# Norm statistics of six stage openings: on 128 token partitions, spread by a diagonal and a matmul of ones

## The chip, the cores and the metric

The kernel runs on one core of one Trainium2 chip. The metric is the device time of one execution in microseconds (us). It is one large program: three transformer-like blocks behind one another on 512 tokens of 1024 channels, in float32, with each weight product made from two float32r parts (a high part and the rest).

## What is computed

Each block is a chain of mixer and feed-forward stages, and most of them open with a root-mean-square norm over the 1024 channels of a token, often followed by a modulation with a shift and a scale:

```python
def rms_norm_3(x, w):
    xf = x.astype(jnp.float32)
    y = xf * lax.rsqrt(jnp.mean(xf * xf, axis=-1, keepdims=True) + EPS)
    return (y * w.astype(jnp.float32)).astype(x.dtype)

def modulate(h, shift, scale):
    return h * (1 + scale) + shift
```

At the seam from the second to the third block two norms follow one another: the second block ends with `norm_f_w_2`, and the third opens with `norm1_w_3` on its result.

## The kernel before

The residual x lies in on-chip memory as `core.x`, 128 partitions x 8 channel tiles x 512 tokens: channels are on partitions, tokens in the free dimension. The stage ahead of a norm leaves `core.sumsq` (128 x 512), the squares of x added over the 8 channel tiles; what is still missing is the sum over the 128 partitions. (The first mixer makes its squares itself, from x as it is loaded.)

Six stages open with such a norm: the first mixer (`stage_first_mixer`), the three feed-forward stages (`stage_ffn`; called FFN1, FFN2 and FFN3 here), the opening of the second block (`stage_delta_rows`, called delta) and the opening of the third block (`stage_third_begin`, called begin). The first five use the class `Norm`, begin has the same steps written out for its two norms. The steps of `Norm`, by engine:

- TensorE (PE), L415: a matmul of a 128 x 128 matrix of ones with `sumsq`. It sums over the partitions and leaves the sum of each token on all 128 partitions, in PSUM (128 x 512, `acc`). A float32 matmul shows as two records in the trace. Behind it `keep_warm` (L290) issues 6 or 7 more matmuls of constants, whose result nobody reads. They have no waits.
- VectorE (DVE), L463 and L465: mean plus epsilon, then the reciprocal, both on 128 x 512.
- ScalarE (ACT), L428: the square root, on 128 x 512.
- DVE, L474: for each of the 8 channel tiles k, x times the gain times `rstd`, into one of three buffers; ACT, L434 or L436, makes the high part of the stage's input from it, and DVE, L447 or L449, the low part. DVE's order is scale 0, scale 1, low part 0, scale 2, low part 1, and so on. Each low part raises `lesser`.
- PE then waits for `lesser` tile by tile and works off the first two weight pieces (`pair`, L278), six matmuls for each channel tile. From there on it goes on through the stage's other pieces.

Each engine works in the order of its own program. ACT has other work ahead of the square root: it makes the high parts (L368) of the first weight pieces, 2 or 4 of them, each as soon as its load has landed. GpSimd (POOL) makes the low parts of the same pieces (L375), each 128 x 1024, and reads them from on-chip memory. Between two stages POOL also clears the semaphores of the stage that has ended. All stages end with a barrier of all engines.

In begin, PE sums `sumsq` and `sumsq2` (L2956, L2957), DVE works the two norms together (L3027 to L3034), and ACT takes the root (L2987). `root` serves the opening of the third block; the second statistic, `gains`, is inverted (L3045) and rooted (L2993) behind the 8 channel tiles, and used later, when x itself is scaled. PE's order is the two sums, `keep_warm`, the pair of `rows_.tensor(2)`, then `gates.tensor(0)` (L2838), then the next rows. ACT's order behind the 8 high parts is two weight pieces, the root of `gains`, and only then `rows_.scalar(1)`, which takes the first result of the pair out of PSUM.

## Time and profile before

| | us |
|---|---|
| median of 3 runs | 3575.83 |
| lowest, highest | 3573.02, 3578.72 |
| span of the profiled execution | 3572.5 |

The three runs are the timed ones; the profiled execution has a span of its own, from its first to its last instruction, and no other time is listed for it. The profile's page gives the busy time of each engine, the chain of waits and the groups of instructions. The timeline gives single instructions or runs of equal ones: start, duration, engine, line, operation and, in square brackets, how long the engine had been idle and what ended that. The stretches (windows) give busy times and the clock granted to TensorE, where 1.00 is 2.4 GHz and 0.50 is 1.2 GHz.

### The profile page before, as it was taken

Reading aid. Unit: us, or ns where it says so; the run is one execution under the profiler, and the core shown is the slowest. Engines: PE = TensorE matmul, PEld = TensorE weight load, DVE = VectorE, ACT = ScalarE, POOL = GpSimd, SP = SyncE. Lnnn points to the kernel's source line nnn. Section 1 sums busy time; section 2 is a strip of 40 time slices with the busy share of each in tenths; the row PEclk is TensorE's granted clock in tenths of the full one; section 3 lists DMA queues with packets and bytes.
Section 4 is the critical chain, followed back from the end, with each engine's and each line's share of the span. In section 5 each row is a group of like instructions: output and inputs, shape, how many; then the busy total and the mean of one; then the engine's idle time right before and its main releaser. Section 6 shows DMA issues by size and latency. Waiting matters only on the chain. (4 is left out here: it accounts for less than half of the span.)

```text
span 3572.5 us, 44627 instructions
## 1 busy us (share of the span) xinstructions
PE 3280.6 (92%) x17750; PEld 2615.2 (73%) x17750; DVE 2137.5 (60%) x2499; ACT 1255.3 (35%) x1906; POOL 1363.7 (38%) x625
## 2 busy tenths in 40 slices
PE   8999999999998899989999998979988758799997
PEld 5778777888766678967888867757876536678885
DVE  6586775889755575344746474867973677531012
ACT  4333433323244323233323342333432544332222
POOL 3434353444332234333444343326631222334442
PEclk9999999999999999999999999989999878899999
DMA  3223353474332246353444132423324555422322
GB/s 118 89 89 126 119 189 117 161 250 153 114 126 83 92 133 167 117 173 136 143 158 140 61 120 98 147 81 125 102 103 129 172 152 162 136 83 83 106 86 68
DMA packets 237262, 447.06 MB, mean 125 GB/s; under 512 B 59792, under 2 KB 119888, under 8 KB 230272
## 3 DMA queue, kind: packets, MB, share of 16 engines
q1 hardware_dynamic: 229984, 433.73, 37.5%
q10 hardware_dynamic: 7072, 10.49, 0.8%
q8 instruction: 141, 2.31, 0.3%
q14 instruction: 65, 0.53, 0.1%
HBM read 394.78 MB, written 49.37 MB: 124 GB/s over the span
## 5 line engine op out<-in xcount | busy, mean ns | idle before, releaser
L375 POOL TENSOR_TENSOR third_feed_lo<-third_feed_raw,third_feed_hi 128x1024 fp32r<-128x1024 f32 (+3 forms) x191 | 449.2, 2355 | 801.0 <-ACT third_feed_hi L368 783.0
L375 POOL TENSOR_TENSOR second_feed_lo<-second_feed_raw,second_feed_hi 128x1024 fp32r<-128x1024 f32 (+3 forms) x182 | 405.6, 2230 | 656.9 <-ACT second_feed_hi L368 627.7
L375 POOL TENSOR_TENSOR first_feed_lo<-first_feed_raw,first_feed_hi 128x1024 fp32r<-128x1024 f32 (+4 forms) x182 | 394.8, 2173 | 560.4 <-ACT first_feed_hi L368 550.6
L273 PE MATMUL shared_ps<-third_h_hi,third_feed_hi 128*128 128x512 f32 (+1 forms) x776 | 324.2, 418 | 55.5 <-ACT lgate_rows_out L894 11.9
L274 PE MATMUL shared_ps<-third_h_lo,third_feed_hi 128*128 128x512 f32 (+1 forms) x776 | 312.5, 403 | 0.0
L275 PE MATMUL shared_ps<-third_h_hi,third_feed_lo 128*128 128x512 f32 (+1 forms) x776 | 312.3, 402 | 0.0
L368 ACT ACTIVATE third_feed_hi<-third_feed_raw 128x1024 fp32r<-128x1024 f32 (+3 forms) x191 | 190.6, 1001 | 297.2 <-PE ffn_low L275 79.1
L368 ACT ACTIVATE second_feed_hi<-second_feed_raw 128x1024 fp32r<-128x1024 f32 (+3 forms) x182 | 173.9, 956 | 206.6 <-PE ffn_low L275 70.8
L368 ACT ACTIVATE first_feed_hi<-first_feed_raw 128x1024 fp32r<-128x1024 f32 (+4 forms) x182 | 168.7, 929 | 209.8 <-PE mixer_acc L275 80.5
L273 PE MATMUL mixer_acc<-first_h_hi,first_feed_hi 128*128 128x512 f32 x544 | 220.5, 405 | 7.5 <-DVE first_h_lo L1578 4.8
L273 PEld LDWEIGHTS shared_ps<-third_h_hi,third_feed_hi 128*128 128x128 f32 (+1 forms) x776 | 152.3, 196 | 100.8 <-issue 64.7
L537 DVE SCALAR_TENSOR_TENSOR ffn_ada_sum<-ffn_ada_w,cond,ffn_ada_sum 128x512 f32<-128x512 f32 x196 | 219.2, 1134 | 4.0
L275 PE MATMUL mixer_acc<-first_h_hi,first_feed_lo 128*128 128x512 f32 x544 | 213.0, 392 | 0.0
L274 PE MATMUL mixer_acc<-first_h_lo,first_feed_hi 128*128 128x512 f32 x544 | 212.8, 391 | 0.0
L725 DVE TENSOR_TENSOR ffn_mid_lo<-ffn_gate,ffn_mid_hi 128x512 fp32r<-128x512 f32 x66 | 113.3, 1716 | 120.8 <-ACT ffn_mid_hi L661 119.4
L274 PEld LDWEIGHTS shared_ps<-third_h_lo,third_feed_hi 128*128 128x128 f32 (+1 forms) x776 | 152.5, 197 | 32.9 <-issue 2.5
L275 PEld LDWEIGHTS shared_ps<-third_h_hi,third_feed_lo 128*128 128x128 f32 (+1 forms) x776 | 151.5, 195 | 33.9
L273 PE MATMUL scans_ps<-delta_in_h_hi,second_feed_hi 128*128 128x512 f32 (+1 forms) x376 | 155.5, 414 | 14.0 <-PEq L1937 6.1
L274 PE MATMUL scans_ps<-delta_in_h_lo,second_feed_hi 128*128 128x512 f32 (+1 forms) x376 | 150.1, 399 | 0.0
L275 PE MATMUL scans_ps<-delta_in_h_hi,second_feed_lo 128*128 128x512 f32 (+1 forms) x376 | 149.9, 399 | 0.0
L273 PE MATMUL ffn_acc<-first_h_hi,first_feed_hi 128*128 128x512 f32 x352 | 138.4, 393 | 1.9 <-DVE first_h_lo L447 1.9
L273 PE MATMUL ffn_acc<-second_h_hi,second_feed_hi 128*128 128x512 f32 x352 | 137.4, 390 | 1.4 <-DVE second_h_lo L449 1.4
(773 smaller groups left out, 8024.5 us busy)
## 6 DMA issues: line engine op xcount, KB each, us to landing
third_feed_raw<-in_stream SPq DMA_DIRECT2D x156, 512.0 KB, 3.4
second_feed_raw<-in_stream SPq DMA_DIRECT2D x130, 512.0 KB, 3.5
first_feed_raw<-in_stream SPq DMA_DIRECT2D x120, 512.0 KB, 3.3
ffn_ada_w<-in_w_ada SPq DMA_DIRECT2D x48, 1024.0 KB, 5.3
shared_seg<-scratch_cum SPq DMA_DIRECT2D x32, 512.0 KB, 7.2
scratch_gates<-mixer_gate ACTq DMA_DIRECT2D x32, 256.0 KB, 2.1
mix_gin<-scratch_gates SPq DMA_DIRECT2D x32, 256.0 KB, 3.1
first_feed_raw<-in_stream SPq DMA_DIRECT2D x28, 256.0 KB, 3.2
```

What stands on the lines that cost most here:

```text
L273: nc.tensor.matmul(out, w_hi, x_hi, start=start, stop=False)
L274: nc.tensor.matmul(out, w_hi, x_lo, start=False, stop=False)
L275: return nc.tensor.matmul(out, w_lo, x_hi, start=False, stop=stop)
L368: self.nc.scalar.activation(self.hi[:, p % self.cut, :n], self.raw[:, p % self.deep, :n], ACT.Copy).then_inc(self.cut_hi, 1)
L375: eng.tensor_tensor(self.lo[:, p % self.cut, :n], self.raw[:, p % self.deep, :n], self.hi[:, p % self.cut, :n].bitcast(F32), ALU.subtract) ...
L537: v.scalar_tensor_tensor(out=at, in0=w, scalar=by, in1=at, op0=ALU.mult, op1=ALU.add).then_inc(self.summed, 1)
L725: v.tensor_tensor(mid_lo[:, f % HALF], gate[:, f % 2], mid_hi[:, f % HALF].bitcast(F32), ALU.subtract).then_inc(done_mid, 1)
```

## The change

The sum over partitions is taken the other way round. `token_sums` makes four matmuls for the four groups of 128 tokens: `sumsq` of the group is now the stationary matrix and a single column of ones is streamed, so the sums of 512 tokens arrive as 128 x 4, tokens on partitions. DVE's mean and reciprocal and ACT's root work on 128 x 4 (`small`). Then `diagonal` multiplies the identity (128 x 128, read for each of the four groups) by `small` (each value read 128 times), a DVE operation of 128 x 512, and a matmul of ones with that diagonal puts the statistic of every token on all partitions again, in `acc` in PSUM. DVE's scaling reads `acc` in place of `rstd` in on-chip memory.

PE's queue gets a wait for the diagonal (`turned`) between two groups of `keep_warm` of two matmuls each, in place of the 6 or 7 in a row. Each norm gets two more semaphores. In begin both statistics go this way: the opening's diagonal as in `Norm`; that of `gains` is made by DVE behind scale 1, its matmul of ones stands on PE behind the pair and ahead of `gates.tensor(0)`, and ACT copies the result out of PSUM at the place where it took the root.

```diff
+def token_sums(nc, core, to, squares):
+    for c in range(4):
+        last = nc.tensor.matmul(to[:, c:c + 1], squares[:, c * P:(c + 1) * P], core.ones[:, 0:1], start=True, stop=True)
+    return last
+
+def diagonal(nc, core, to, by):
+    return nc.vector.tensor_tensor(to.rearrange("p (c t) -> p c t", c=4), core.ident[:].unsqueeze(1).broadcast_to([P, 4, P]),
+                                   by.unsqueeze(2).broadcast_to([P, 4, P]), ALU.mult)
 class Norm:
-    def tensor(self, pe):
+    def tensor(self, pe, warm):
-        self.nc.tensor.matmul(self.acc, self.core.ones[:], self.core.sumsq[:], start=True, stop=True
-                              ).then_inc(self.summed, 1)
+        token_sums(self.nc, self.core, self.acc, self.core.sumsq).then_inc(self.summed, 1)
+        keep_warm(self.nc, self.core, warm, 2)
+        pe.wait_ge(self.turned, 1)
+        self.nc.tensor.matmul(self.acc, self.core.ones[:], self.rstd[:], start=True, stop=True).then_inc(self.wide, 1)
+        keep_warm(self.nc, self.core, warm, 2)
...
-        self.nc.scalar.activation(self.rstd[:], self.rstd[:], ACT.Sqrt).then_inc(self.rooted, 1)
+        self.nc.scalar.activation(self.small[:], self.small[:], ACT.Sqrt).then_inc(self.rooted, 1)
...
-        v.tensor_scalar(self.rstd[:], self.acc, 1.0 / D, EPS, ALU.mult, ALU.add).then_inc(self.meaned, 1)
+        v.tensor_scalar(self.small[:], self.acc[:, 0:4], 1.0 / D, EPS, ALU.mult, ALU.add).then_inc(self.meaned, 1)
-        v.reciprocal(self.rstd[:], self.rstd[:]).then_inc(self.inverted, 1)
+        v.reciprocal(self.small[:], self.small[:]).then_inc(self.inverted, 1)
         dve.wait_ge(self.rooted, 1)
+        diagonal(self.nc, core, self.rstd[:], self.small[:]).then_inc(self.turned, 1)
+        dve.wait_ge(self.wide, 1)
...
-            v.scalar_tensor_tensor(out=to, in0=core.x[:, k], scalar=g[:, k:k + 1], in1=self.rstd[:], op0=ALU.mult,
-                                   op1=ALU.mult).then_inc(self.scaled, 1)
+            v.scalar_tensor_tensor(out=self.buf[:, k % 3], in0=core.x[:, k], scalar=g[:, k:k + 1], in1=self.acc,
+                                   op0=ALU.mult, op1=ALU.mult).then_inc(self.scaled, 1)
 stage_ffn, stage_first_mixer, stage_delta_rows
-            norm.tensor(pe)
-            keep_warm(nc, core, acc[:, 1], 7)
+            norm.tensor(pe, acc[:, 1])
 stage_third_begin, PE
+                token_sums(nc, core, ps[:, 4], core.sumsq).then_inc(summed, 1)
+                token_sums(nc, core, ps[:, 5], core.sumsq2).then_inc(summed, 1)
+                keep_warm(nc, core, ps[:, 1], 2)
+                pe.wait_ge(spread_, 1)
+                nc.tensor.matmul(ps[:, 5], core.ones[:], root[:], start=True, stop=True).then_inc(wide, 1)
+                keep_warm(nc, core, ps[:, 1], 2)
                 rows_.tensor(pe, 2)
+                pe.wait_ge(spread_, 2)
+                nc.tensor.matmul(ps[:, 4], core.ones[:], gains, start=True, stop=True).then_inc(wide, 1)
                 gates.tensor(pe, 0)
 stage_third_begin, ACT
-                act.wait_ge(inverted, 2)
-                a.activation(gains, gains, ACT.Sqrt).then_inc(rooted, 1)
+                act.wait_ge(wide, 2)
+                a.activation(gains, ps[:, 4], ACT.Copy).then_inc(rooted, 1)
 stage_third_begin, DVE, in the loop over c
+                    if c == 1:
+                        diagonal(nc, core, gains, small[:, 4:8]).then_inc(spread_, 1)
                     if c:
                         lesser_part(c - 1)
...
-                v.reciprocal(gains, gains).then_inc(inverted, 1)
```

## Rows read from the trace of the kernel before

**Rows 1.** The page, part 1: engine, busy us (share of span), instructions.

```profile
PE 3280.6 (92%) x17750; PEld 2615.2 (73%) x17750; DVE 2137.5 (60%) x2499; ACT 1255.3 (35%) x1906; POOL 1363.7 (38%) x625
```

**Rows 2.** Timeline of FFN1's opening: start, us, engine, line, operation [idle <-releaser].

```profile
582.41 1.98 PE L415 MATMUL ffn_total<-sumsq,ones 128*128 128x512 f32 x2 [2.46 <-PEq L1192]
584.19 6.16 PE L293 MATMUL ffn_ada_acc<-pick,ones 128*128 128x512 f32 x12
585.16 3.35 DVE L465 RECIPROCAL ffn_norm_rstd<-ffn_norm_rstd 128x512 f32<-128x512 f32 x1
587.80 2.35 POOL L375 TENSOR_TENSOR first_feed_lo<-first_feed_raw,first_feed_hi 128x1024 fp32r<-128x1024 f32 x1 [9.65 <-issue]
589.21 2.15 DVE L474 SCALAR_TENSOR_TENSOR ffn_norm_buf<-x_res,vec,ffn_norm_rstd 128x512 f32<-128x512 f32 x2 [0.70 <-ACT ffn_norm_rstd L428]
592.24 0.47 PE L273 MATMUL ffn_acc<-first_h_hi,first_feed_hi 128*128 128x512 f32 x1 [1.88 <-DVE first_h_lo L447]
```

**Rows 3.** Timeline of the first mixer's opening.

```profile
14.96 2.07 PE L415 MATMUL mixer_out<-sumsq,ones 128*128 128x512 f32 x2 [14.96 <-DVE sumsq L490]
20.13 4.65 POOL L375 TENSOR_TENSOR first_feed_lo<-first_feed_raw,first_feed_hi 128x1024 fp32r<-128x1024 f32 x2
22.35 1.28 ACT L428 ACT_TABLE_LOAD   x1
24.31 1.68 DVE L474 SCALAR_TENSOR_TENSOR mix_norm_buf<-x_res,vec,mix_norm_rstd 128x512 f32<-128x512 f32 x2 [3.16 <-ACT mix_norm_rstd L428]
26.87 0.47 PE L273 MATMUL mixer_acc<-first_h_hi,first_feed_hi 128*128 128x512 f32 x1 [2.64 <-DVE first_h_lo L447]
```

**Rows 4.** Timeline of delta's opening.

```profile
982.25 4.66 POOL L375 TENSOR_TENSOR second_feed_lo<-second_feed_raw,second_feed_hi 128x1024 fp32r<-128x1024 f32 x2 [21.54 <-ACT second_feed_hi L368]
983.54 1.28 ACT L428 ACT_TABLE_LOAD   x1
985.50 2.61 DVE L474 SCALAR_TENSOR_TENSOR slots_a<-x_res,delta_norm_full,slots_a 128x512 f32<-128x512 f32 x2 [1.37 <-ACT slots_a L428]
989.14 0.47 PE L273 MATMUL scans_ps<-delta_in_h_hi,second_feed_hi 128*128 128x512 f32 x1 [2.19 <-DVE delta_in_h_lo L449]
```

**Rows 5.** Timeline of begin's opening.

```profile
2061.22 4.85 POOL L375 TENSOR_TENSOR third_feed_lo<-third_feed_raw,third_feed_hi 128x1024 fp32r<-128x1024 f32 x2 [20.36 <-ACT third_feed_hi L368]
2062.53 1.28 ACT L2987 ACT_TABLE_LOAD   x1
2068.67 1.41 DVE L3040 SCALAR_TENSOR_TENSOR begin_buf<-x_res,begin_full,begin_root 128x512 f32<-128x512 f32 x2 [0.70 <-ACT begin_root L2987]
2071.11 0.77 PE L273 MATMUL shared_ps<-third_h_hi,third_feed_hi 128*128 128x512 f32 x1 [4.55 <-DVE third_h_lo L3018]
```

**Rows 6.** Timeline of FFN2's opening, then of FFN3's.

```profile
1681.51 1.42 DVE L474 SCALAR_TENSOR_TENSOR ffn_norm_buf<-x_res,ffn_norm_full,ffn_norm_rstd 128x512 f32<-128x512 f32 x2 [0.70 <-ACT ffn_norm_rstd L428]
...
3172.78 7.01 PE L293 MATMUL ffn_ada_acc<-pick,ones 128*128 128x512 f32 x12
3173.02 2.35 POOL L375 TENSOR_TENSOR third_feed_lo<-third_feed_raw,third_feed_hi 128x1024 fp32r<-128x1024 f32 x1 [5.46 <-ACT third_feed_hi L368]
3177.83 1.41 DVE L474 SCALAR_TENSOR_TENSOR ffn_norm_buf<-x_res,ffn_norm_full,ffn_norm_rstd 128x512 f32<-128x512 f32 x2 [0.70 <-ACT ffn_norm_rstd L428]
```

**Rows 7.** PE's timeline: single-column matmuls, full then half clock; two records of `keep_warm`.

```profile
970.06 1.84 PE L552 MATMUL ffn_ada_acc<-ones,ffn_ada_sum 128*128 128x1 f32 x16
974.95 2.23 PE L552 MATMUL ffn_ada_acc<-ones,ffn_ada_sum 128*128 128x1 f32 x10
1681.58 1.02 PE L293 MATMUL ffn_ada_acc<-pick,ones 128*128 128x512 f32 x2
```

**Rows 8.** Single lines over the run: durations in ns, least/median/most.

```profile
L1887 DVE TENSOR_SCALAR delta_bias<-vec x1: 164/164/164, 978.1 to 978.1; 128x4 f32<-128x4 f32 x1
L4238 DVE TENSOR_TENSOR ssm_xw<-ssm_xdt,ssm_w x24: 680/684/2852, 2771.3 to 3025.5; 128x512 f32<-128x512 f32 x24
```

**Rows 9.** A stretch of FFN1: busy times (PE to POOL), then granted clock, DMA.

```profile
592.80:595.80 3.00, 3.00 (x8) 2.34 (x7) 3.00 (x6) 1.73 (x3) 0.00 (x0) 0.50 0.08 30
```

More of the change, by code:

```diff
@@ L407, in __init__ @@
         self.rstd, self.buf = bufs
+        self.small = s.sb("norm_small", [P, 4])
+        self.turned, self.wide = owner.sem("norm_turned"), owner.sem("norm_wide")
         (self.squared, self.added, self.summed, self.meaned, self.inverted, self.rooted, self.ready, self.scaled,
@@ L427, in scalar @@
         act.wait_ge(self.inverted, 1)
-        self.nc.scalar.activation(self.rstd[:], self.rstd[:], ACT.Sqrt).then_inc(self.rooted, 1)
-        if self.parts is None:
-            return
+        self.nc.scalar.activation(self.small[:], self.small[:], ACT.Sqrt).then_inc(self.rooted, 1)
         for k in range(DT):
@@ L614, in _ @@
                 steps = 0
-                norm.tensor(pe)
-                keep_warm(nc, core, ada_acc[:], 6)
+                norm.tensor(pe, ada_acc[:])
                 for half in range(2):
@@ L1264, in out @@
                 last.then_inc(out_ready, 1)
-            norm.tensor(pe)
-            keep_warm(nc, core, acc[:, 1], 7)
+            norm.tensor(pe, acc[:, 1])
             pair(pe, feed, ROWS1[:2], norm.lesser, (acc[:, 0], acc[:, 1]), h)
@@ L1824, in lora @@
                     last.then_inc(product_, 1)
-                norm.tensor(pe)
-                keep_warm(nc, core, ps[:, 1], 7)
+                norm.tensor(pe, ps[:, 1])
                 rows_.tensor(pe, 5)
@@ L2901, in stage_third_begin @@
         k, v_ctx, last_ = s.sb("k", [P, 4, CTX]), s.sb("v_ctx", [P, 2, D]), s.sb("last", [P, 2, 4])
-        start = s.sb("start", [P, 2, 256])
+        start, small = s.sb("start", [P, 2, 256]), s.sb("small", [P, 8])
         gates = LogGates(nc, core, s, s, ps[:, 6:8].rearrange("p a (b c) -> p (a b) c", c=CTX), CTX, CTX, b)
@@ L2908, in stage_third_begin @@
         stored = [s.sem(f"stored{n}") for n in range(2)]
-        gained = s.sem("gained")
+        gained, spread_, wide = s.sem("gained"), s.sem("spread"), s.sem("wide")
         with nc.Block() as block:
@@ L2954, in state @@
                     last.then_inc(product_, 1)
-                nc.tensor.matmul(ps[:, 4], core.ones[:], core.sumsq[:], start=True, stop=True).then_inc(summed, 1)
-                nc.tensor.matmul(ps[:, 5], core.ones[:], core.sumsq2[:], start=True, stop=True).then_inc(summed, 1)
-                keep_warm(nc, core, ps[:, 1], 7)
+                token_sums(nc, core, ps[:, 4], core.sumsq).then_inc(summed, 1)
[4 more added lines that the diff above has]
+                keep_warm(nc, core, ps[:, 1], 2)
                 rows_.tensor(pe, 2)
+                pe.wait_ge(spread_, 2)
+                nc.tensor.matmul(ps[:, 4], core.ones[:], gains, start=True, stop=True).then_inc(wide, 1)
                 gates.tensor(pe, 0)
@@ L2986, in _ @@
                 act.wait_ge(inverted, 1)
-                a.activation(root[:], root[:], ACT.Sqrt).then_inc(rooted, 1)
+                a.activation(small[:], small[:], ACT.Sqrt).then_inc(rooted, 1)
                 for c in range(DT):
@@ L3026, in _ @@
                 dve.wait_ge(summed, 2)
-                v.tensor_scalar(gains, ps[:, 4], 1.0 / D, EPS, ALU.mult, ALU.add).then_inc(meaned, 1)
+                v.tensor_scalar(small[:, 4:8], ps[:, 4, 0:4], 1.0 / D, EPS, ALU.mult, ALU.add).then_inc(meaned, 1)
                 dve.wait_ge(meaned, 1)
-                v.tensor_scalar(root[:], gains, EPS, None, ALU.mult).then_inc(meaned, 1)
+                v.tensor_scalar(small[:, 0:4], small[:, 4:8], EPS, None, ALU.mult).then_inc(meaned, 1)
                 dve.wait_ge(meaned, 2)
-                v.scalar_tensor_tensor(out=root[:], in0=ps[:, 5], scalar=1.0 / D, in1=root[:], op0=ALU.mult,
-                                       op1=ALU.add).then_inc(meaned, 1)
+                v.scalar_tensor_tensor(out=small[:, 0:4], in0=ps[:, 5, 0:4], scalar=1.0 / D, in1=small[:, 0:4],
+                                       op0=ALU.mult, op1=ALU.add).then_inc(meaned, 1)
                 dve.wait_ge(meaned, 3)
-                v.reciprocal(root[:], root[:]).then_inc(inverted, 1)
+                v.reciprocal(small[:], small[:]).then_inc(inverted, 1)
                 dve.wait_ge(rooted, 1)
+                diagonal(nc, core, root[:], small[:, 0:4]).then_inc(spread_, 1)
                 dve.wait_ge(ready, 2)
+                dve.wait_ge(wide, 1)
                 for c in range(DT):
@@ L3039, in _ @@
                         dve.wait_ge(lesser, c - 2)
-                    v.scalar_tensor_tensor(out=buf[:, c % 3], in0=core.x[:, c], scalar=full[:, c:c + 1], in1=root[:],
+                    v.scalar_tensor_tensor(out=buf[:, c % 3], in0=core.x[:, c], scalar=full[:, c:c + 1], in1=ps[:, 5],
                                            op0=ALU.mult, op1=ALU.mult).then_inc(scaled, 1)
+                    if c == 1:
+                        diagonal(nc, core, gains, small[:, 4:8]).then_inc(spread_, 1)
                     if c:
```

14 lines of the change are left out of this document (5 added, 9 removed).

## Prediction

> **What bounds the kernel now.** I read the page first: TensorE (PE) is busy for 92% of the span, so a stage costs what PE needs for it plus what PE stands still [rows 1]. A norm that opens a stage is such a standstill. PE's own operation, the sum, is followed by constant matmuls that nobody needs, and the first weight matmul comes only when DVE has made the first low part: at 26.87, 592.24, 989.14 and 2071.11, each with an idle time that a low part ended [rows 2 to 5]. Behind it PE has work without a break, so what the first weight matmul comes earlier or later is what the stage ends earlier or later. I therefore follow that one instruction through six openings, in the timeline.
>
> In FFN1 the chain is plain: sum at 582.41, first scale at 589.21, 6.80 later, of which the reciprocal alone is 3.35 [rows 2]. The reader should see that the other openings are not all like this. In the first mixer and in delta the root stands behind ACT's weight pieces and its table load, which ends at 22.35 + 1.28 = 23.63 and 983.54 + 1.28 = 984.82, while the scales start at 24.31 and 985.50, only one root later [rows 3, 4]. There the reciprocal is not what comes last. In begin the table load ends at 2063.81, and the root, one root's time ahead of the scale at 2068.67, starts 4.2 later: it could move so far, not more [rows 5].
>
> **Prices of the new steps.** Four single-column matmuls are eight records. Sixteen took 1.84 at full clock (8: 0.92), ten took 2.23 at half clock (8: 1.78) [rows 7]. A DVE operation of 128x4 takes 0.164 [rows 8], so mean and reciprocal are about 0.4 with their handovers; the root of 128x4 I put at 0.2, its old 0.63 being the upper bound (the scale's start less the table's end). The diagonal is a DVE tensor_tensor of 128x512 with two on-chip operands, one of them a broadcast: the nearest row is L4238, of that form, at 0.68, but with cases of 2.85 [rows 8]. What such a case is can be seen in delta: its first two scales, two on-chip operands too, took 2.61 in place of begin's 1.41, so the first was done at about 985.50 + 0.75 + 1.20 = 987.45, which is 0.54 behind the end of POOL's low parts at 982.25 + 4.66 = 986.91 [rows 4, 5]. So bounds 0.7 free, POOL's end + 0.54 held; where POOL is at work I take held, since two forms show it. The wide matmul of ones is two records: 1.02 at full clock [rows 7], 1.98 at half [rows 2]. Between the sums and it PE has four constant records: 1.72 at full clock (1.02 less the overlap, 0.43 each), 3.4 at half.
>
> After the first scale nothing changes in size: the first low part and first weight matmul follow 2.56 later in the mixer, 2.44 in begin [rows 3, 5]. In FFN1 it was 3.03, the first scales being slowed by POOL (2.15 for two) [rows 2]. Reading `acc` from PSUM I cost at nothing.
>
> **Opening by opening.**
> - First mixer. Root at 23.65 as before, done 23.85. POOL's last low part runs to 24.78 [rows 3], so the diagonal is done at 25.3 instead of 24.6. PE, with 1.8 + 3.4 of sums and constants from 14.96 at most, has stood for five microseconds then, so I take the wide matmul at half clock: 27.4, against a first scale at 24.31 [rows 3]. Loss 3.1. Bounds: 1.3 (free, full clock) to 5.1 (half clock also through the four constants behind it, 0.5, and through three microseconds of the pair, 1.5).
> - Delta. Root done at 985.05, POOL until 986.91 [rows 4], diagonal 987.45, wide at half clock 989.4; plus 2.5 is 991.9 against 989.14. Loss 2.8; bounds 0.1 to 4.9.
> - FFN1. The constants show the clock: twelve records in 6.16 where full clock would need 5.3, so the first two ran at half, until shortly before 586 [rows 2]. New: sums to 584.2, mean and reciprocal 584.6, root 584.8 or, behind the table load, somewhat later, diagonal by 586 (POOL starts only at 587.80). But four constant records from 584.2, two at half and two at full clock, run until 586.8. Wide until 587.9: first scale 1.3 earlier. The first low part then falls under POOL's piece (587.80 + 2.35 = 590.15, about 0.2 later by more semaphores to clear), so the first weight matmul comes at 591.0: gain 1.2. In the profile the clock fell behind that gap and stayed at half from 592.8 to 595.8, which cost 1.5 [rows 9]; the constants behind the wide matmul leave a gap no longer than before's 1.88 [rows 2], so I count half of it, 0.8. Gain 2.0; bounds -0.5 to 2.8.
> - FFN2. The same without a table load and with the diagonal held until about PE's constants end: gain 1.4 of the scale's start at 1681.51 [rows 6]; bounds -0.4 to 1.8.
> - FFN3. POOL holds from 3173.02 to 3175.37, diagonal 3175.9, wide partly in the half-clock stretch that the constants show there (7.01 for twelve records, so four at half), to 3177.5 against 3177.83 [rows 6]. Gain 0.3; bounds -0.3 to 1.2.
> - Begin. Two sums; statistics done by 2061.3; root at 2063.85, done 2064.05; POOL until 2066.07 [rows 5], diagonal 2066.6, wide at half clock 2068.6: nothing gained against 2068.67. The second diagonal, in DVE's queue between scale 1 and the first low part, holds that low part and with it PE by 0.7. The pair began at half clock (0.77 for its first matmul, 0.47 elsewhere) [rows 3, 5], which for a stretch like FFN1's [rows 9] is worth 1.5; half of that, 0.7, comes back if PE is kept busy. The second wide matmul then stands on PE's own path, 1.0. Its readers, ACT's copy and the rows queued behind that, were late behind the second reciprocal before and are no later relative to PE. That reciprocal (3.35 on DVE) was hidden beside PE's pair and gives nothing. Loss 0.9 (the 0.7 for the diagonal, 1.0 for the matmul, less 0.7 and 0.1); bounds -2.3 to +2.5.
>
> Sum: -3.1 - 2.8 + 2.0 + 1.4 + 0.3 - 0.9 = -3.1, so 3.1 us slower: a span of 3575.6 against 3572.5. What lies around the span is 3.3 by the median of the runs (3575.83), which gives 3578.9. Bounds added up: 6.9 faster to 13.5 slower.
>
> **A rule on the clock.** After 4.55 us without a matmul begin's pair ran at half clock; after 2.64 in the mixer the first weight matmul (0.47, against 0.77 in begin) ran at full [rows 3, 5]. The Trainium skill, "TensorE: Matmul & The Clock Gate", section "HAM oscillation — how this bites in real kernels", says that PE which idles between bursts is throttled again, so that each burst begins cold; begin agrees, the mixer does not. By that rule alone the second rival would be the forecast.
>
> **Rivals.**
> 1. The short chain counts everywhere. If sums, four small steps, diagonal and wide were all that stood between PE's start and the first scale, at 1.8 + 0.4 + 0.3 + 0.7 + 2.0 = 5.2 at half clock or 3.4 at full against 6.8, each of six openings would gain about 2: 3564. For it: FFN1's chain, with 3.35 in one reciprocal. Against it: the table loads in mixer and delta, POOL in four of six, PE's own constants. Chance 0.05.
> 2. The new wait makes stage openings cold. PE stands before `turned` with its constants spent; wide, the constants behind it and the pair's first three microseconds run at half clock. Price 1.5 for the pair and 0.5 for the constants in an opening, nothing saved of the 1.5 that I credited: in all six about 12 more, 3591. Three openings suffice to make it slower by more than 0.2%: 3.1 + 1.5 + 3 x 2 is over 7. For it: PE idles some 5 us in mixer, delta and begin. Against it: the gap ahead of the pair, 2.6 in the mixer before, shrinks to about 1. Chance 0.12.
> 3. DVE isn't held by POOL. Diagonals then come 0.7, 1.7 and 1.8 earlier in mixer, delta and begin: 3574.7. For it: most rows of L4238 are 0.68. Chance 0.15.
> 4. The norm isn't on the path at all, so nothing changes: excluded by PE's idle times ahead of the first weight matmul.
>
> **How the numbers follow.** The forecast, gains and losses that nearly cancel, has 0.63, the rest of 0.05 lies outside all of these. The predicted time is 3579. The range takes in rival 3 and three quarters of rival 2 and is a little narrower than the added bounds: 3570 to 3588. About 0.2% (7 us) is what a measurement can tell from no change. Faster by more: rival 1 and little else, 0.06. Slower by more: rival 2 and the forecast's own tail, 0.15. Within: 0.79.
>
> **What would show it.** The first weight matmul in the mixer near 30 and in delta 2 to 3 later than before relative to its stage's start; the diagonal there ending about half a microsecond behind POOL's low part, at more than 0.7. In FFN1 and FFN2 the first scale 1 to 1.5 earlier, its matmul started at the end of the constants and not of the diagonal. In begin the first weight matmul hardly moved, and the gates' matmuls a microsecond further behind the pair. Wrong would be: an opening of mixer or delta that gains, a diagonal of 0.7 while POOL runs, or a clock that decides more than 1.5 in most openings.

## The result, and the profile after

The changed kernel took 3587.13 us (median of 6 runs, 3584.49 to 3588.86) against 3575.51 for the kernel before (6 runs of the same measurement, 3573.02 to 3579.79). The ratio is 1.0029, with a 95% interval of 1.0019 to 1.0040: about 10 us slower by the ratio. Measured a second time, among the experiments, it was 3584.25 against 3578.82, ratio 1.0016 (1.0007 to 1.0025), some 6 us slower. So it is slower, by about the 0.2% that the prediction gives as what a measurement can tell from no change. The profiled execution had a span of 3584.3 us, against 3572.5.

The page hardly moved. Part 1 of the page (engine, busy us and share of the span, instructions), which answers to [rows 1]:

```profile
PE 3288.3 (92%) x17776; PEld 2624.1 (73%) x17776; DVE 2127.0 (59%) x2505; ACT 1251.6 (35%) x1906; POOL 1364.6 (38%) x625
```

DVE had 10.5 us less work, and the span still grew: in most openings the time that DVE saved was not what the stage waited for. The openings show why. First mixer, timeline of the changed kernel (start, us, engine, line, operation, idle time before it and what ended that), for comparison with [rows 3]:

```profile
15.44 1.86 PE L300 MATMUL mixer_out<-ones,sumsq 128*128 128x1 f32 x8 [15.44 <-DVE sumsq L503]
15.76 9.27 POOL L388 TENSOR_TENSOR first_feed_lo<-first_feed_raw,first_feed_hi 128x1024 fp32r<-128x1024 f32 x4 [10.06 <-ACT first_feed_hi L381]
17.34 0.16 DVE L479 TENSOR_SCALAR mix_norm_small<-mixer_out 128x4 f32<-128x4 f32 x1 [1.96 <-PE mixer_out L300]
22.54 1.28 ACT L446 ACT_TABLE_LOAD   x1
23.83 0.21 ACT L446 ACTIVATE mix_norm_small<-mix_norm_small 128x4 f32<-128x4 f32 x1
24.07 1.51 DVE L306 TENSOR_TENSOR mix_norm_rstd<-ident,mix_norm_small 128x512 f32<-128x512 f32 x1 [6.36 <-ACT mix_norm_small L446]
25.63 2.08 PE L433 MATMUL mixer_out<-mix_norm_rstd,ones 128*128 128x512 f32 x2 [4.71 <-DVE mix_norm_rstd L306]
27.75 1.41 DVE L488 SCALAR_TENSOR_TENSOR mix_norm_buf<-x_res,vec,mixer_out 128x512 f32<-128x512 f32 x2 [2.17 <-PE mixer_out L433]
30.13 1.42 PE L273 MATMUL mixer_acc<-first_h_hi,first_feed_hi 128*128 128x512 f32 x1
```

The mean is ready at 17.5, and the root comes at 23.83, behind ACT's four weight pieces and the table load, as before. DVE stood idle for 6.36 ahead of the diagonal, where it had stood for 3.16 ahead of the scales [rows 3]: the 3.2 by which these differ is what the short statistics saved, spent waiting. From the end of the root (24.04) on there are now two steps more: the diagonal, done at 25.58, and the wide matmul at half clock, done at 27.71. Delta, against [rows 4], has the same form:

```profile
987.12 4.65 POOL L388 TENSOR_TENSOR second_feed_lo<-second_feed_raw,second_feed_hi 128x1024 fp32r<-128x1024 f32 x2 [22.45 <-ACT second_feed_hi L381]
988.40 1.28 ACT L446 ACT_TABLE_LOAD   x1
989.93 2.38 DVE L306 TENSOR_TENSOR slots_a<-ident,delta_norm_small 128x512 f32<-128x512 f32 x1 [4.79 <-ACT delta_norm_small L446]
992.37 2.07 PE L433 MATMUL scans_ps<-slots_a,ones 128*128 128x512 f32 x2 [4.38 <-DVE slots_a L306]
996.91 1.20 PE L273 MATMUL scans_ps<-delta_in_h_hi,second_feed_hi 128*128 128x512 f32 x1
```

FFN1, against [rows 2], is the opening that gained. The chain has lost the long reciprocal; the wide matmul now follows the end of the constants (594.47), not that of the diagonal (593.76):

```profile
590.27 1.02 PE L300 MATMUL ffn_total<-ones,sumsq 128*128 128x1 f32 x8 [2.45 <-PEq L1204]
591.15 3.32 PE L293 MATMUL ffn_ada_acc<-pick,ones 128*128 128x512 f32 x4
593.07 0.69 DVE L306 TENSOR_TENSOR ffn_norm_rstd<-ident,ffn_norm_small 128x512 f32<-128x512 f32 x1 [1.36 <-ACT ffn_norm_small L446]
594.26 1.41 PE L433 MATMUL ffn_total<-ffn_norm_rstd,ones 128*128 128x512 f32 x2
598.36 0.47 PE L273 MATMUL ffn_acc<-first_h_hi,first_feed_hi 128*128 128x512 f32 x1 [0.97 <-DVE first_h_lo L463]
```

Begin, against [rows 5], and FFN3, against [rows 6]. Begin's statistics are done early, its root again waits for the pieces and the table load (2070.08 + 1.28), and the diagonal and the wide matmul fill what the reciprocal left. In FFN3 the sums (1.84) and all four constants (3.76) run at half clock, and the wide matmul starts 1.19 behind the end of its diagonal:

```profile
2063.77 3.54 PE L300 MATMUL shared_ps<-ones,sumsq 128*128 128x1 f32 x16 [3.90 <-PEq L610]
2071.62 1.81 DVE L306 TENSOR_TENSOR begin_root<-ident,begin_small 128x512 f32<-128x512 f32 x1 [3.47 <-ACT begin_small L3003]
2073.48 2.08 PE L2970 MATMUL shared_ps<-begin_root,ones 128*128 128x512 f32 x2 [2.55 <-DVE begin_root L306]
2078.49 0.47 PE L273 MATMUL shared_ps<-third_h_hi,third_feed_hi 128*128 128x512 f32 x1 [0.73 <-DVE third_h_lo L3034]
...
3182.84 1.84 PE L300 MATMUL ffn_total<-ones,sumsq 128*128 128x1 f32 x8 [2.50 <-PEq L1098]
3184.54 3.76 PE L293 MATMUL ffn_ada_acc<-pick,ones 128*128 128x512 f32 x4
3185.44 1.47 DVE L306 TENSOR_TENSOR ffn_norm_rstd<-ident,ffn_norm_small 128x512 f32<-128x512 f32 x1 [0.27 <-ACT ffn_norm_small L446]
3188.10 1.55 PE L433 MATMUL ffn_total<-ffn_norm_rstd,ones 128*128 128x512 f32 x2
3192.12 0.47 PE L273 MATMUL ffn_acc<-third_h_hi,third_feed_hi 128*128 128x512 f32 x1 [0.76 <-DVE third_h_lo L465]
```

To compare kernels I measure each opening from the start of its sums to the start of its first weight matmul, in the timeline. "Sum" is the six together against before; "between" is the rest of the span against before, stretches whose code is the same in all kernels but for the second statistic of begin, behind its pair, and for a matmul that copies the identity to PSUM in two of them; the ratio is that of the timed runs to those of the kernel before, with its interval. The names of the lower rows are explained with the experiments. The copy of the identity stands ahead of the sums and so is not in the lengths: 0.30 to 0.56 us in each opening but the mixer's, 2.0 us in all with the identity in PSUM and 2.3 in the last kernel. Each trace is of one execution, and not always of one near the median: the second of the changed kernel is its slowest (3587.81 against 3584.25), those of the identity in PSUM and of the last kernel are their fastest (3578.30 against 3584.00, 3562.60 against 3565.82), so "between" is that execution's and not the kernel's.

| kernel | mixer | FFN1 | delta | FFN2 | begin | FFN3 | sum | between | ratio |
|---|---|---|---|---|---|---|---|---|---|
| before | 11.91 | 9.83 | 11.24 | 9.29 | 14.21 | 8.42 | | | |
| before, 2nd trace | 11.89 | 9.83 | 11.47 | 9.28 | 14.08 | 8.93 | +0.6 | -2.5 | 0.9995 (0.9986 to 1.0004) |
| after | 14.69 | 8.09 | 14.08 | 7.87 | 14.72 | 9.28 | +3.8 | +8.0 | 1.0029 (1.0019 to 1.0040) |
| after, 2nd trace | 14.61 | 8.09 | 14.27 | 9.50 | 14.31 | 9.52 | +5.4 | +8.0 | 1.0016 (1.0007 to 1.0025) |
| old statistics in two | 11.79 | 9.35 | 11.24 | 7.96 | 14.51 | 9.26 | -0.8 | +3.2 | 0.9995 (0.9985 to 1.0004) |
| identity in PSUM | 14.08 | 8.29 | 11.88 | 7.80 | 14.59 | 7.80 | -0.5 | +4.4 | 1.0012 (1.0001 to 1.0023) |
| more constants | 14.44 | 8.58 | 14.06 | 7.88 | 14.82 | 7.90 | +2.8 | +7.0 | 1.0010 (0.9999 to 1.0022) |
| root first | 11.09 | 8.09 | 9.83 | 7.85 | 11.81 | 9.46 | -6.8 | +8.8 | 0.9990 (0.9980 to 1.0000) |
| before, root first | 11.22 | 9.82 | 13.41 | 9.37 | 14.18 | 8.42 | +1.5 | +10.6 | 1.0010 (1.0001 to 1.0019) |
| root first, PSUM, one constant | 10.39 | 8.28 | 9.28 | 7.38 | 10.88 | 7.81 | -10.9 | -0.9 | 0.9967 (0.9955 to 0.9978) |

### The profile page after: what moved, and what is told of

Its sections match the earlier page's. It is cut to its first block and busy times, and to the rows that moved or that the text cites. A ratio compares the mean times of both kernels' runs of the same rounds, so it can differ in the third digit from the quotient of the medians.

```text
span 3584.3 us, 44698 instructions
## 1 busy us (share of the span) xinstructions
PE 3288.3 (92%) x17776; PEld 2624.1 (73%) x17776; DVE 2127.0 (59%) x2505; ACT 1251.6 (35%) x1906; POOL 1364.6 (38%) x625
```

## The experiments

**The statistics of before in the first mixer and delta alone.** `Norm` gets a switch, set for these two stages:

```diff
+        if self.plain:
+            self.nc.tensor.matmul(self.acc, self.core.ones[:], self.core.sumsq[:], start=True, stop=True
+                                  ).then_inc(self.summed, 1)
+            keep_warm(self.nc, self.core, warm, 7)
+            return
...
+        to = self.rstd if self.plain else self.small
...
-        norm = Norm(nc, core, s, outer, "mix_norm", out_[:], h, None, x_loaded)
+        norm = Norm(nc, core, s, outer, "mix_norm", out_[:], h, None, x_loaded, plain=True)
```

> The 128x512 statistics of the kernel before, with its seven constants, come back in the first mixer and the delta stage alone; the other four openings stay as changed. Theory A, the two openings with the long chain lose the time: the trace of after shows the first mixer's opening 4.4 us later than before and the delta's 3.4 us later, so this kernel is 7 to 8 us shorter than the changed one (about 3579.5 us) and some 4 us longer than the one before. Theory B, most of the loss comes from half-clock stretches at places whose code is the same (3.4 us later between the mixer's opening and FFN1, 2 us in the last third): then putting two openings back shortens it by under 4 us, or moves it without proportion, and the half-clock stretches before FFN1 stay.

Measured: 3580.55, ratio 0.9995. Theory A, but for one thing: the two openings are back at before's lengths, and the whole loss is gone, where some 4 us over before had been expected to stay. Against the changed kernel that is 0.2 to 0.3%, 7.5 to 12 us by the two ratios of that one, where the two openings had 5.7 us; the half-clock start of the two pairs (1.42 and 1.20 above, 0.47 twice here) goes with them. Of theory B this much holds: up to FFN1 this kernel's first mixer has the steps and the constants of before, and yet the stretch from there to FFN1's sums took 557.11 us, where before's two traces have 555.54 and 556.88 (the changed kernel's 560.1 and 558.3). So that stretch varies by 1.6 us without the change.

**The identity in PSUM.**

```diff
     def tensor(self, pe, warm):
+        self.nc.tensor.matmul(self.acc[:, P:2 * P], self.core.ident[:], self.core.ident[:], start=True, stop=True)
...
-        diagonal(self.nc, core, self.rstd[:], self.small[:]).then_inc(self.turned, 1)
+        diagonal(self.nc, core, self.rstd[:], self.small[:], self.acc[:, P:2 * P]).then_inc(self.turned, 1)
```

> One more matmul copies the identity into free columns of the sums' bank, and the diagonal reads it there, so that it has one operand in SBUF in place of two. Theory A, the diagonal is long because POOL works beside it: it falls from 1.51 (first mixer), 2.38 (delta), 1.81 (begin), 2.18 and 1.47 us (FFN2, FFN3) to about 0.7 us at all of them; that is worth 0.8 + 1.7 + 1.1 us, less about 0.2 us for the extra matmul at each, and nothing at FFN2 and FFN3, where the constants hold the wide matmul: 3 us shorter than the changed kernel. Theory B, it is the operation itself that varies (its broadcasts): it stays at 1.5 to 2.4 us, and the time is the same within 1 us.

The diagonal's line over the whole run (durations in ns, least/median/most, then the starts of the first and the last), first in the changed kernel:

```profile
L306 DVE TENSOR_TENSOR ffn_norm_rstd<-ident,ffn_norm_small x3: 693/1468/2178, 593.1 to 3185.4; 128x512 f32<-128x512 f32 x3
L306 DVE TENSOR_TENSOR slots_a<-ident,delta_norm_small x1: 2379/2379/2379, 989.9 to 989.9; 128x512 f32<-128x512 f32 x1
```

and the same groups with the identity in PSUM, with POOL's pieces in delta there:

```profile
L306 DVE TENSOR_TENSOR ffn_norm_rstd<-ffn_total,ffn_norm_small x3: 691/692/693, 591.7 to 3178.1; 128x512 f32<-128x512 f32 x3
L306 DVE TENSOR_TENSOR slots_a<-scans_ps,delta_norm_small x1: 692/692/692, 989.2 to 989.2; 128x512 f32<-128x512 f32 x1
...
986.39 4.65 POOL L388 TENSOR_TENSOR second_feed_lo<-second_feed_raw,second_feed_hi 128x1024 fp32r<-128x1024 f32 x2 [22.16 <-ACT second_feed_hi L381]
```

Theory A: 0.69 at all openings, in delta in the midst of POOL's work (986.39 to 991.04), with the same broadcasts. What held the diagonal beside POOL was its second operand in on-chip memory (SBUF), not its form. The openings were 4.3 us shorter than in the changed kernel's first trace, 2.3 with the copies (expected 3). Delta gave what was expected. Begin did not: its diagonal was short too, but ACT's first weight piece, behind a load, came 4.66 after the start of the sums in place of 3.33, and the root stood behind it. FFN3 gained 1.5 where nothing was expected, its sums having run at full clock this time (0.95 in place of 1.84). The time, 3584.00 (1.0012), lies between before's and the changed kernel's; its interval doesn't separate it from the second measurement of the latter. The Trainium skill, "SBUF — State Buffer", section "Who interferes with whom", states this as a rule: a DVE instruction with two inputs in SBUF contends with a GpSimd instruction that reads SBUF; one with at most one such input does not, outside the modes in which DVE uses both of its port pairs. These rows agree, with 0.69 against up to 2.38.

**More constants ahead of the wait.**

```diff
-            norm.tensor(pe, acc[:, 1])
+            norm.tensor(pe, acc[:, 1], 8, 2)
-                norm.tensor(pe, ps[:, 1])
+                norm.tensor(pe, ps[:, 1], 7, 2)
-                keep_warm(nc, core, ps[:, 1], 2)
+                keep_warm(nc, core, ps[:, 1], 5)
                 pe.wait_ge(spread_, 1)
```

> Eight constants in place of two ahead of the wait for the diagonal in the first mixer, seven in delta, five in begin, so that PE works through the time in which it waited idle 4.71, 4.38 and 2.55 us there. Theory A, the wide matmul runs at the half clock (2.08, 2.07 and 2.08 us) because PE stood idle ahead of it: it falls to about 1.0 us in the three places, and the first weight matmuls start at the full clock: 2 to 2.5 us each in the mixer and delta, 1 us in begin, about 5 us in all. Theory B, more constants only push the wide matmul out behind them (they run at the half clock at 1.8 us each): 0 to 4 us longer than the changed kernel.

PE and the diagonal in the first mixer:

```profile
17.64 9.54 PE L293 MATMUL mixer_acc<-pick,ones 128*128 128x512 f32 x16
24.59 1.42 DVE L306 TENSOR_TENSOR mix_norm_rstd<-ident,mix_norm_small 128x512 f32<-128x512 f32 x1 [6.40 <-ACT mix_norm_small L446]
27.01 1.02 PE L433 MATMUL mixer_out<-mix_norm_rstd,ones 128*128 128x512 f32 x2
30.35 0.47 PE L273 MATMUL mixer_acc<-first_h_hi,first_feed_hi 128*128 128x512 f32 x1 [0.60 <-DVE first_h_lo L463]
```

Both theories hold by half. The wide matmul and the first weight matmul are at full clock (1.02 and 0.47, in delta too, 1.11 and 0.47 in begin). But the constants end at 27.18, after the diagonal's end at 26.01, and the wide matmul, which would have started then, starts at 27.01. The mixer's opening is 0.25 shorter than in the changed kernel, delta's the same, begin's 0.1 longer, where 5 us in all had been expected; the time is 3584.63 (1.0010). Kept busy, PE is warm and late; left idle, it is cold and early; here these came out alike.

**The root first.** In the first mixer it comes behind two weight pieces and not behind all four, in delta and begin ahead of them:

```diff
             feed.split_hi(act, 2)
+            norm.scalar_root(act)
             feed.split_hi(act, feed.cut)
-            norm.scalar(act)
+            norm.scalar(act, False)
...
+                norm.scalar_root(act)
                 feed.split_hi(act, 2)
-                norm.scalar(act)
+                norm.scalar(act, False)
...
-                feed.split_hi(act, 2)
                 act.wait_ge(inverted, 1)
                 a.activation(small[:], small[:], ACT.Sqrt).then_inc(rooted, 1)
+                feed.split_hi(act, 2)
```

> ACT takes its root ahead of the weight pieces that stood before it: after the first two pieces in the mixer, ahead of all of them in delta and begin. Theory A, what the short statistics save is lost because the root waits for ACT's weight pieces and not for the statistics (mean at 17.34, root at 23.83 us in the mixer; the root of delta 5 us behind its sums): the scales start 4 to 5 us earlier in the mixer and in delta and about 3 us earlier in begin, 10 to 12 us in all, which gives about 3575 us, as before or a little shorter. Theory B, the pieces moved behind the root now come late for the first weight matmul, and the end of the opening stays with them: 0 to 4 us shorter than the changed kernel.

Measured: 3576.38, ratio 0.9990 (0.9980 to 1.0000), where the changed kernel had 1.0029 and 1.0016: clearly faster than that one, and just at the edge of what can be told from before. The first mixer with the root first:

```profile
15.31 9.73 POOL L388 TENSOR_TENSOR first_feed_lo<-first_feed_raw,first_feed_hi 128x1024 fp32r<-128x1024 f32 x4 [9.72 <-ACT first_feed_hi L381]
17.79 0.20 ACT L446 ACTIVATE mix_norm_small<-mix_norm_small 128x4 f32<-128x4 f32 x1
18.02 2.49 DVE L306 TENSOR_TENSOR mix_norm_rstd<-ident,mix_norm_small 128x512 f32<-128x512 f32 x1 [1.09 <-ACT mix_norm_small L446]
23.96 1.63 DVE L467 TENSOR_TENSOR first_h_lo<-mix_norm_buf,first_h_hi 128x512 fp32r<-128x512 f32 x1
25.74 0.47 PE L273 MATMUL mixer_acc<-first_h_hi,first_feed_hi 128*128 128x512 f32 x1 [1.54 <-DVE first_h_lo L467]
```

Theory A by 10.6 us in the openings: mixer 3.6, delta 4.3, begin 2.9 shorter than in the changed kernel. The root waits for the table load and the statistics now, the pieces are no longer ahead of it. What is late next shows too: the first low part took 1.63 in place of 0.69, until 25.59, half a microsecond behind POOL's end (25.04); delta's took 0.94. In these two it is not the pieces moved behind the root that the first weight matmul waits for, as theory B had it, but DVE, held by POOL.

**The root first in the kernel before**, in the mixer and delta, by the same edit there.

> The kernel before with ACT's root ahead of the weight pieces in the first mixer and delta, and the 128x512 statistics kept. Theory A, the short statistics are worth their saving once the root is early: here the root still waits for the 3.35 us reciprocal, so the mixer's opening gains at most 2.5 us and delta's at most 0.9, where the short ones gained 3.6 and 4.3 us by the same move; 0 to 3.4 us under the kernel before. Theory B, the order of the root is what counts and the form of the statistics does not: this comes out as fast as the changed kernel with the root first, about 0.1% under the kernel before.

Neither theory: 3583.38, ratio 1.0010, a little slower than before. Delta:

```profile
987.33 0.63 ACT L428 ACTIVATE slots_a<-slots_a 128x512 f32<-128x512 f32 x1 [5.03 <-DVE slots_a L469]
988.99 5.38 POOL L375 TENSOR_TENSOR second_feed_lo<-second_feed_raw,second_feed_hi 128x1024 fp32r<-128x1024 f32 x2 [25.76 <-ACT second_feed_hi L368]
990.50 1.68 DVE L453 SCALAR_TENSOR_TENSOR delta_in_h_lo<-slots_a,mod,delta_in_h_hi 128x512 fp32r<-128x512 f32 x1 [1.09 <-ACT delta_in_h_hi L440]
994.47 0.77 PE L273 MATMUL scans_ps<-delta_in_h_hi,second_feed_hi 128*128 128x512 f32 x1 [3.35 <-POOL second_feed_lo L375]
```

The scales start 6.93 behind the sums instead of 7.60, but ACT's pieces now wait for the root, POOL's pieces for ACT, and the first weight matmul for POOL (988.99 + 5.38): 13.41 in place of 11.24. With the reciprocal in the chain the pieces had better not wait for the root: before's order, pieces first [rows 4], is the faster one there. In the mixer, where two pieces stay ahead of the root, the same move gained 0.7 (11.22), against 3.6 with the short statistics. So in delta the form of the statistics and the place of the root have to change together, and in the mixer they do more together than the root's move alone.

**Both kernels once more**, unchanged, each for a second trace.

> The kernel before once more, for a second trace and a ratio that should be 1. Theory A, the first trace of before had few half-clock stretches between the openings by chance: its openings repeat within 0.5 us and the stretches between them come out 2 to 6 us longer. Theory B, the stretches between are steady in this kernel: they repeat within 1.5 us in sum, and the 3 to 9 us by which all five other kernels are longer there belong to the change.

> The changed kernel once more, for a second trace of it. The six openings, from the first sums to the first weight matmul, were together 3.8 us longer than before in its first trace, and the stretches between them, whose code is the same, 8.0 us. Theory A, the between part is mostly where the half-clock stretches happened to fall: the openings repeat within 1 us (mixer +2.8, delta +2.8, FFN1 -1.7, FFN2 -1.4, begin +0.5, FFN3 +0.9 against before), while the stretches between them change by several us and in other places. Theory B, the changed openings make what follows them slower: the same stretches come out long again, above all the one from the first mixer's opening to FFN1 (+4.6 us, with 15 us more at the half clock), and the loss stays near 0.3%.

Before against itself: 0.9995. Its openings repeat within 0.6 us in sum, and the stretches between came out 2.5 shorter, not longer. Theory A had the sign wrong; that they move by more than 1.5 without any change was right. The changed kernel's openings repeat to about 0.2 in four cases and to 0.4 in begin; FFN2 came out 1.6 longer, its sums at 1.70, its constants at 3.76 and its wide matmul at 1.91, all at half clock, in place of 1.13, 3.55 and 1.02. Between, it is 8.0 longer again, as theory B had it, but in other places, as theory A had it: from the mixer to FFN1 2.8 in place of 4.6, from delta to FFN2 4.3 in place of 0.7, from begin to FFN3 1.1 in place of 3.6. One such place, between the same two ACT instructions in the first and the second trace of the changed kernel (stretch; us, busy times from PE to POOL, granted clock, DMA share, GB/s), and PE's longest wait in each:

```profile
1370.62:1439.57 68.95, 62.23 (x1135) 58.43 (x1136) 31.33 (x46) 22.47 (x40) 32.64 (x19) 0.93 0.71 185
...
1369.21:1441.80 72.59, 62.08 (x1123) 58.04 (x1125) 31.45 (x46) 22.36 (x39) 30.72 (x19) 0.91 0.68 179
```

```profile
1382.85 1.97 PE L1755 MATMUL scans_ps<-slots_a,x_res 64*64 64x64 f32 x32 [5.86 <-PEq L2185]
...
1383.71 1.97 PE L1755 MATMUL scans_ps<-slots_a,x_res 64*64 64x64 f32 x32 [8.14 <-PEq L2185]
```

PE was busy for 62 us in both. What differs is its idle time, 6.7 and 10.5, of which this one wait has 2.3 more, and with it the clock. Before took 69.74 there with a wait of 6.13, before with the root first 72.98 with one of 8.40. So the same code comes in a short and a long form, in kernels with the change and without it, and of two traces of one kernel one is of each kind. What makes the wait longer in one than in the other was not followed.

**Root first, identity in PSUM, and one constant.** The last of the edits is `keep_warm(..., 1)` in place of 2 ahead of each wait for the diagonal.

> Root first, the identity in PSUM, and one constant in place of two ahead of each wide matmul. With the root early, the diagonal (held by POOL, 2.49 us in the mixer) and the two constants (3.76 us at the half clock; the wide matmul of delta came 1.94 us behind the end of its diagonal) are what is late next. Theory A: the wide matmul follows the diagonal at once, which against the kernel with the root first alone takes 2.7 us from the mixer's opening, 1.7 from delta's, 1.5 from begin's, 0.8 from FFN1's and 1.6 from FFN2's and FFN3's, less 0.3 us at each for the extra matmul: about 8 us, and some 10 us or 0.3% under the kernel before. Theory B, PE then idles more and its clock falls: the wide matmuls and the first weight matmuls run at the half clock, and all of it is given back.

Measured: 3565.82 (6 runs) against 3578.82, ratio 0.9967 (0.9955 to 0.9978): faster than both kernels, by 0.33% and by about 0.5 to 0.6%. The openings are 10.9 shorter than before's, 8.6 with the copies of the identity. Both theories show. The wide matmul follows the end of the diagonal within 0.3 everywhere, and it is at half clock everywhere, 1.91 to 2.08. So against the kernel with the root first, the copies left out, FFN1 lost 0.2 and FFN2 gained 0.5, where gains of 0.8 and 1.6 had been expected, and FFN3's 1.65 is no more than the identity in PSUM had with two constants (7.80). First mixer, POOL and the first low part:

```profile
15.92 9.28 POOL L388 TENSOR_TENSOR first_feed_lo<-first_feed_raw,first_feed_hi 128x1024 fp32r<-128x1024 f32 x4 [10.29 <-ACT first_feed_hi L381]
23.13 2.62 DVE L468 TENSOR_TENSOR first_h_lo<-mix_norm_buf,first_h_hi 128x512 fp32r<-128x512 f32 x1 [0.31 <-ACT first_h_hi L455]
25.89 0.47 PE L273 MATMUL mixer_acc<-first_h_hi,first_feed_hi 128*128 128x512 f32 x1 [2.80 <-DVE first_h_lo L468]
```

Of the 2.7 expected in the mixer 0.7 came: the low part, with both operands in on-chip memory, starts earlier and waits for POOL's end (25.20) all the same. POOL's low parts are what bounds this opening now. All six openings together are 4.1 shorter than with the root first, 1.9 with the copies, where about 8 had been expected. The time came out as expected all the same, some 8 us by the two ratios; three quarters of that lie between the openings, and no run tells what made them. Nor was the share of the identity separated from that of the one constant.

## Why the prediction was right or wrong

The time lies within the range, near its upper end. The upper end had been put there for pairs at half clock, and that is not what brought the time there: the openings show the likeliest case, a small loss within 0.2%, and most of what the first measurement has above it lies outside of them, where the forecast had no term. To that extent it is luck that the range held. The second measurement is within 0.2%. A small term was off too: what lies around the span was put at 3.3, from the median of other executions; where one execution has both numbers it is 1.9 (3586.16 less 3584.3).

The forecasts below are those up to the first weight matmul, which is what the openings measure; behind it I had counted another +0.8 in FFN1 and -0.3 in begin. The bounds are those of the whole opening, with what lies behind it.

| gain (+) or loss (-), us | forecast | bounds | first trace | second trace |
|---|---|---|---|---|
| first mixer | -3.1 | -5.1 to -1.3 | -2.8 | -2.7 |
| delta | -2.8 | -4.9 to -0.1 | -2.8 | -3.0 |
| FFN1 | +1.2 | -0.5 to +2.8 | +1.7 | +1.7 |
| FFN2 | +1.4 | -0.4 to +1.8 | +1.4 | -0.2 |
| FFN3 | +0.3 | -0.3 to +1.2 | -0.9 | -1.1 |
| begin | -0.6 | -2.3 to +2.5 | -0.5 | -0.1 |
| sum | -3.6 | | -3.8 | -5.4 |

That the first trace's sum agrees to 0.2 is in part chance: FFN1 and the mixer are 0.8 better than forecast, FFN3 is 1.2 worse.

- *What stands behind the root.* Right: mixer, delta and begin keep their root where it was. Moving only ACT's root recovered 10.6 us of openings, which is the shown cause of the loss there. Rival 1, some 2 us gained in each of six openings, shows in FFN1 and FFN2 alone.
- *The diagonal held by POOL.* Right, and to a tenth of a microsecond: it ended 0.55 and 0.54 behind POOL's low part in mixer and delta (25.58 against 25.03, 992.31 against 991.77), where the forecast took 0.54. Rival 3 fell with it. The identity in PSUM shows that it is the operand, not the operation.
- *The wide matmul.* Right in mixer, delta and begin (2.07 or 2.08 at half clock). In FFN1 and FFN2 it waited for the constants, as forecast, until 594.47 and 1687.63.
- *FFN1.* It gained 1.7 ahead of the first weight matmul, 0.5 more than forecast: the scales read PSUM now and took 1.41 beside POOL in place of 2.15 [rows 2], which I had costed at nothing. Behind it the half-clock stretch of [rows 9] is gone, so that nearly the whole 1.5 came back and not half of it (the stretch from there to delta's sums is 1.2 shorter), about 3 in all and beyond the bound of 2.8. The stretch that answers to [rows 9] in the changed kernel (its second trace has the same clock):

```profile
598.40:601.40 3.00, 3.00 (x13) 2.48 (x14) 3.00 (x6) 1.27 (x2) 0.00 (x0) 1.00 0.83 299
```

- *FFN3, the wrong sign, and FFN2 in the second trace.* The step that failed is that the wide matmul follows the diagonal. The diagonal ended 4.07 behind the start of the sums, as forecast (3175.9 less 3171.85). But the sums (1.84) and the four constants (3.76) ran at half clock from end to end and held PE until 5.46, 1.4 later, and the wide matmul, partly cold itself (1.55), ended at 6.81 where I had 5.65. The second trace has the same in FFN3 and in FFN2. I had put PE's constants into the sum of FFN1 and FFN2 and left them out here. In before's first trace FFN3's sums had run at full clock:

```profile
3171.85 1.10 PE L415 MATMUL ffn_total<-sumsq,ones 128*128 128x512 f32 x2 [2.50 <-PEq L1086]
```

  A cold start is not new (before's second trace has 1.60 there, and FFN1 starts cold in [rows 2]), but it costs the new form more. Over all traces six FFN openings with the old statistics began cold, the sums taking 1.60 to 2.05, and all were back at full clock within three of the twelve constants; seven with the new ones did, 1.46 to 1.84 (about 1.0 at full clock), and none was back before the wide matmul. What makes a start cold is not shown.
- *Begin.* To the first weight matmul as forecast. The second diagonal's 0.68 ahead of the first low part is there, and the pair started at full clock (0.47 against 0.77 [rows 5]), though PE had again been idle, for 2.55, ahead of the wide matmul. What lies behind came out otherwise. The second wide matmul does hold the gates by 0.95 (to 2090.42), and the pair, warm, is 1.5 shorter, so they come 0.6 earlier behind the pair's start. But the premise that PE has work without a break from there on did not hold: some 8 us behind the gates' start PE waits for ACT, in before for 1.52 and now for 2.12, and comes to the same place (21.7 behind the pair's start in both). Here are the second wide matmul and the first matmul behind that wait, then the latter in before:

```profile
2089.47 1.02 PE L2974 MATMUL shared_ps<-shared_spare,ones 128*128 128x512 f32 x2
2100.21 0.67 PE L273 MATMUL shared_ps<-third_h_hi,third_feed_hi 128*128 128x512 f32 x1 [2.12 <-ACT third_merged L902]
...
2092.80 0.47 PE L273 MATMUL shared_ps<-third_h_hi,third_feed_hi 128*128 128x512 f32 x1 [1.52 <-ACT third_merged L890]
```

  In the first trace PE came out of the longer wait at half clock (0.67), and the last of the gates' matmuls came 36.0 behind the pair's start in place of 34.4; in the second trace it did not (34.4).
- *Cold pairs, rival 2.* It came in two openings of six, and for less than its price of 1.5: the first weight matmul took 1.42 in the mixer and 1.20 in delta (0.69 and 1.00 in the second trace), 0.95 and 0.73 over [rows 3, 4], and by the fourth matmul the pairs had lost 1.1 and 0.7. The first 3.5 us of delta's pair had a clock of 0.87, where before had 1.00:

```profile
996.91:1000.41 3.50, 3.50 (x14) 2.53 (x13) 3.50 (x6) 1.76 (x3) 0.00 (x0) 0.87 0.03 11
```

  The rule that I cited from "TensorE: Matmul & The Clock Gate", section "HAM oscillation — how this bites in real kernels", of the Trainium skill, that bursts after an idle time begin cold, agrees with delta, whose constants had come back to full clock (3.46 for four) and whose wide matmul, after 4.38 of idle, was at half (2.07). The wide matmuls of the mixer and begin (both 2.08) say little, since PE was at half clock there from the sums on (the constants 3.76 in both), and begin's pair was at full clock.

What the sum lacked. The openings give 3.8 and 5.4 us of a measured loss of 10.4 and 5.7. The rest is time outside of them. There PE was busy 5.6 us longer than in before, and idle 2.3 longer; the mean clock, 0.961 before and 0.956 after, says that more of the span was at half: (1 - 0.961) x 2 x 3572.5 = 279 us and (1 - 0.956) x 2 x 3584.3 = 315. The cold pairs of mixer and delta (1.1 and 0.7) don't explain it, since FFN1's warm one gives 1.2 back. One place that belongs to the change is PE's wait in begin, with 1.6 us lost at half clock behind it in the first trace. For the rest the runs show that such stretches move without a change: 2.5 us between before's two traces, up to 3.6 in single stretches between the changed kernel's two. From the mixer to FFN1 PE was busy 545.3 and 543.6 in the changed kernel and 538.2 and 540.4 in before, but 543.5 with the old statistics in that mixer. The timed ratios follow the openings' sums, with the copies of the identity, within about 3 us in eight of nine cases; in the first measurement of the changed kernel they are 6.6 apart. Each ratio is uncertain by some 3 to 4 us. That the changed openings also make later stretches longer, by two or three microseconds, isn't excluded: all traces but that of the last kernel and before's second are longer there than before's first. But so is that of before with the root first, whose FFNs, begin and statistics are unchanged. It stays open.

## What to carry to other kernels

A shorter step pays only if what waits for its result was waiting for it: look at what the engine behind it has in its own queue, here weight pieces and a table load ahead of the root, and move the queue together with the step. Either one alone lost time here; both together took the openings 6.8 us under before's and the time 0.1% (at the edge of the noise), and with the next two holders the time was 0.33% under, of which the openings show 8.6 us. A chain with more hand-overs also has more places where another engine can hold it, and what was hidden (a low part held by POOL, a constant at half clock) becomes the next bound. On effects of a few microseconds compare the same stretch in the trace of several kernels, and take two traces of the same one, before reading a single span.

## What the runs showed of the hardware

- A DVE operation with two operands in on-chip memory (SBUF) that meets POOL's work ends 0.54 to 0.55 us behind the end of the POOL operation then running (diagonals 25.58 to 25.03 and 992.31 to 991.77; low parts 25.59 to 25.04 and 25.75 to 25.20), also where one operand is a broadcast of 128 x 4 values. With one of them in PSUM it takes 0.69 beside the same POOL work.
- It also works the other way a little: two of POOL's pieces took 4.65 to 4.67 in most openings [rows 3, 4], and 5.38 and 5.43 in before with the root first, where DVE's scales and low parts stood among them.
- Reading the scale's second operand from PSUM frees it from POOL: two scales took 1.41 beside POOL's work in FFN1 (from 595.71, POOL 595.30 to 597.67), against 2.15 and 2.61 before [rows 2, 4]. I had costed that at nothing.
